# TensorE's program order in the token mix of a two-layer decoder step: where a block's scores stand among the key transposes and the side pieces

## The chip, the cores and the metric

One core of a Trainium2 chip runs the whole step as one program. The metric is the device time of one execution, in microseconds (us), median of several runs.

## What is computed

The reference is a decoder trunk of two layers for a prompt of 256 tokens and for 8 sequences of 8 new tokens each, with 1,024 cached positions per sequence in pages of 128. Each layer is

```
x += 0.5*SwiGLU(RMSNorm(x))
h = RMSNorm(x); project h to queries, keys, values, gates
(A) block-sparse attention, 6 heads: each query keeps the best 3 of the 4 past blocks of 256 keys
(B) forgetting attention, 5 heads: logits get a sum of log forget values
(C) gated linear recurrence, 5 heads
x += concat(A, B, C) @ w_out
x += 0.5*SwiGLU(RMSNorm(x))
```

For the sampled sequences (A) and (B) attend over cached keys and values that are fetched by a page table. The scores of a sequence come in 4 blocks of 256 keys. The softmax of a sequence needs all 4: the sums of the scores pick the block that is left out, and the row maxima give the bias of the exponentials. All of this is in float32.

## The kernel before, in words

The dense products (line 1424) take each weight as a high and a low part. They stand before and after the token mix of each layer, and the change doesn't touch them. The token mix is one unrolled loop over 32 steps, `i` from 0 to 31, on each of TensorE (PE), VectorE (DVE) and ScalarE (ACT). A step is one block of 256 keys: `q, n = divmod(i, 4)`, sequence q, block n of it. Every engine runs its own list of work in exactly the order in which the code gives it, and the lists are tied by semaphores.

TensorE in step i, before the change:

- `turn_keys(i + 1, u)` for u = 0, 1, 2 (line 1588): 12 transposes of cached keys of the next block, 4 in each of three PSUM banks. ACT copies banks 0 and 2 to SBUF (line 688), DVE copies bank 1 (line 1064).
- `block_scores(i)` (lines 1614 and 1618): the scores of this block, into one of four half banks. Blocks 0 and 1 of a sequence write over what the exponentials of the previous sequence read, so block 0 waits until two of its five exponentials are done (line 1614, for line 697).
- n = 1: `turn_weights(q - 1)` (line 1626). n = 2: `values(q - 1)` (line 1643). n = 3: `turn_outputs(q - 1)` (line 1656). These are the previous sequence's softmax weights, its weighted values and its outputs.
- a side piece that belongs to the prompt or to the recurrence. Steps 0 to 13: `prompt_scores(i)` (line 1668), `turn_probs(i - 2)` (line 1680), `prompt_out(i - 3)` (line 1693). Steps 14 to 22: `products(i - 14)` (line 1717). Step 23: `turn_end_keys` (lines 1734 and 1736). Step 24: `rec_own_sums` (line 1748). Steps 25 to 27: state sums, state products and mean squares (line 1795). Steps 28 to 31 have none.

DVE in step i: `block_stats(i - 1)` (lines 1092 and 1093: sum and maximum of the scores), at n = 0 `gates(q - 1)` (lines 1099 to 1105) and `copy_outputs(q - 2)` (line 1143), then `copy_keys(i + 1, 1)` (line 1064), and behind it the work of the side pieces: `prompt_norm(i - 2)`, `prompt_max(i - 1)` (lines 1178 to 1182), `take` and `level_factors` (lines 1223, 1250 and 1251), `level_logs` (line 1244).

ACT in step i: `copy_keys(i + 1, 0)` and `copy_keys(i + 1, 2)` (line 688), then at n = 0 the exponentials `weights(q - 1)` (lines 697 and 699), then `prompt_exp(i - 1)` (line 716), `copy_probs(i - 3)` (line 725), `level_exp` (line 733). ACT's part of the mean squares (lines 760 and 763) stands ahead of its key copies in step 28. In step 23 it copies the cross products (line 748).

So `products(n)` needs DVE's `level_factors(n - 1)` of the same step, `prompt_scores(i)` needs line 1178 of the same step on DVE, and `turn_probs(i - 2)` needs line 725 of the same step on ACT. Each of the three stands behind a key copy of the same step on its engine.

SyncE's queue fetches the key pages (it waits for `keys_turned`), GpSimd's queue the value pages (it waits for `values_used`). The order in which the PSUM banks of the ring are handed out is fixed by `ring_units`, in which block scores don't stand.

Of the kernel before, what the change touches and what calls it, by code (L numbers as in the profile page):

```python
# [239 lines left out]
def trunk(nc, a, outs):  # L240
    ctx = ExitStack()
    with ctx:
# [169 lines left out]
        def settle(eng):  # L412

            eng.sem_inc(waited, 1)
# [998 lines left out]
        def _(te):  # L1413
# [75 lines left out]
            n = DEPTH * 24 + 8  # L1489
# [28 lines left out]
            for L in range(DEPTH):  # L1518
# [38 lines left out]
                def ring(*name):  # L1557

                    if PREVIOUS[name]:
                        te.wait_ge(*was_read(*PREVIOUS[name]))  # L1560
                    settle(te)
                    return ring_bank(*name)
# [16 lines left out]
                def turn_keys(i, u):  # L1579

                    q, n = divmod(i, NBLK)
                    bank = ring(L, "keys", i, u)
                    for j in range(4):
                        a_, pr = divmod(4 * u + j, 6)
                        pg = 2 * n + a_
                        if j == 0 or pr == 0:
                            te.wait_ge(k_in[pg % 4], ((L * DB + q) * 2 + pg // 4) * 32 + 32)
                        last = te.transpose(PS[:, bank, 128 * j:128 * j + 128], key_pages[:, pg % 4, 128 * pr:128 * pr + 128], ident)  # L1588
                    last.then_inc(keys_turned, 1)
# [10 lines left out]
                def block_scores(i):  # L1600

                    q, n = divmod(i, NBLK)
                    Q = L * DB + q
                    for u in range(3):
                        te.wait_ge(*was_read(L, "keys", i, u))
                    if n < 2:
                        if Q:
                            te.wait_ge(weights_ready, 5 * Q - 3 + 2 * n)
                    else:
                        te.wait_ge(block_scores_read, L * BLOCKS + i - 1)  # L1610
                    settle(te)
                    o = [PS[32 * g:32 * g + 32, 3 + n % 2, 256 * (n // 2):256 * (n // 2) + 256] for g in range(3)]
                    for g in (1, 2):
                        te.matmul(o[g], sel[:, q, 32 * g - 32:32 * g], brow[:, 256 * n:256 * n + 256], start=True, stop=False)  # L1614
                    k = keys_t[i % 2][:, :, :].rearrange("p (a j) c -> p j a c", a=2)
                    for m in range(2):
                        for g in range(3):
                            last = te.matmul(o[g], qz[:, q, 2 * g + m, :], k[:, 2 * g + m, :, :], start=g == 0 and m == 0, stop=m == 1)  # L1618
                    last.then_inc(block_scores_done, 1)

                def turn_weights(q):

                    te.wait_ge(weights_ready, (L * DB + q) * 5 + 5)
                    bank = ring(L, "weights", q, 0)
                    for g in range(5):
                        last = te.transpose(PS[:, bank, ROWS * g:ROWS * g + ROWS], weight_rows[:, 128 * g:128 * g + 128], ident[0:ROWS, 0:ROWS])
                    last.then_inc(weights_turned, 1)
                    bank = ring(L, "weights", q, 1)
                    for g in range(3):
                        te.transpose(PS[:, bank, ROWS * g:ROWS * g + ROWS], weight_rows[:, 128 * g + 640:128 * g + 768], ident[0:ROWS, 0:ROWS])  # L1630
                    te.transpose(PS[0:NS, bank, 264:352], new_weights, ident[0:ROWS, 0:ROWS]).then_inc(weights_turned, 1)

                def values(q):

                    Q = L * DB + q
                    for u in range(2):
                        te.wait_ge(*was_read(L, "weights", q, u))
                    bank = ring(L, "values", q)
                    o = [PS[32 * g:32 * g + 32, bank, 0:w] for g, (c, w) in enumerate(GROUPS)]
                    for pg in range(NPG):  # L1640
                        te.wait_ge(v_in[pg], Q * 32 + 32)
                        for g, (c, w) in enumerate(GROUPS):
                            last = te.matmul(o[g], weight_cols[:, pg, 32 * g:32 * g + 32], value_pages[:, pg, c:c + w], start=pg == 0, stop=False, skip_group_check=True)  # L1643
                        last.then_inc(values_used, 1)
                    p, v = [weight_cols[0:NS, NPG, 32 * g:32 * g + 32] for g in range(3)], toks[0:NS, :]
                    te.matmul(o[0], p[0], v[:, 384:640], start=False, stop=True, skip_group_check=True)
                    te.matmul(o[1][:, 0:128], p[1], v[:, 640:768], start=False, stop=True, skip_group_check=True)
                    te.matmul(o[2], p[2], v[:, 3 * 384 + 128:3 * 384 + 320], start=False, stop=True, skip_group_check=True)
                    te.matmul(o[1][:, 128:256], p[1], v[:, 3 * 384:3 * 384 + 128], start=False, stop=True, skip_group_check=True).then_inc(value_sums_ready, 1)

                def turn_outputs(q):

                    te.wait_ge(*was_read(L, "values", q))
                    bank = ring(L, "out", q)
                    for m in range(2):
                        last = te.transpose(PS[:, bank, ROWS * m:ROWS * m + ROWS], out_rows[:, 128 * m:128 * m + 128], ident[0:ROWS, 0:ROWS])
                    last.then_inc(outputs_turned, 1)

                def prompt_scores(h):

                    hf = h % 2
                    r = slice(64 * hf, 64 * hf + 64)
                    qt, kt = pt(T["qa"] + h // 2), pt(T["ka"] + h // 2)
                    if h:
                        te.wait_ge(prompt_scores_read, L * NH + h)
                    for t in range(2):
                        out = PS[:, 5, 128 * t:128 * t + 128 * (t + 1)]
                        last = te.matmul(out, qt[r, 128 * t:128 * t + 128], kt[r, 0:128 * (t + 1)], start=True, stop=h < AH)  # L1668
                        if h >= AH:
                            e = h - AH  # L1670
                            last = te.matmul(out, ident[0:BH, e:e + 1].to_broadcast([BH, 128]), ncn[:, 0:128 * (t + 1)], start=False, stop=True)
                    last.then_inc(prompt_scores_ready, 1)
# [117 lines left out]
                def mean_squares():  # L1790

                    te.wait_ge(rec_squares_ready, L + 1)
                    for j in range(3):
                        bank = ring(L, "squares", j)
                        te.matmul(PS[:, bank, 0:NT], cst("blk"), V_(4, j), start=True, stop=True).then_inc(rec_mean_squares_ready, 1)
# [4 lines left out]
                settle(te)  # L1800
                for i in range(BLOCKS):
                    q, n = divmod(i, NBLK)
                    if i + 1 < BLOCKS:
                        for u in range(3):
                            turn_keys(i + 1, u)
                    block_scores(i)
                    if n == 1 and q >= 1:
                        turn_weights(q - 1)
                    if n == 2 and q >= 1:
                        values(q - 1)  # L1810
                    if n == 3 and q >= 1:
                        turn_outputs(q - 1)
                    if i < NH:
                        prompt_scores(i)
                    if 2 <= i <= NH + 1:
                        turn_probs(i - 2)
                    if 3 <= i <= NH + 2:
                        prompt_out(i - 3)
                    if LEVEL0 <= i <= LEVEL0 + 8:
                        products(i - LEVEL0)  # L1820
                    if i == END0:
                        turn_end_keys()
                    if i == END0 + 1:
                        rec_own_sums()
                    if i == END0 + 2:
                        rec_state_sums()
                        prompt_states()
                    if i == END0 + 3:
                        state_products()
                    if i == END0 + 4:  # L1830
                        mean_squares()
                turn_weights(DB - 1)
                values(DB - 1)
                turn_outputs(DB - 1)
# [57 lines left out]
```

## Time and profile before

| what | value |
|---|---|
| median of 3 runs | 1914.46 us (1908.67 to 1914.79) |
| the profiled execution, device time | 1912.16 us |
| its span, first to last instruction | 1910.5 us |
| TensorE matmul busy | 1755.8 us, 92% |
| VectorE busy | 1100.8 us, 58% |
| ScalarE busy | 638.3 us, 33% |
| mean granted TensorE clock | 0.949 |
| chain that ended last | PE 82%, DVE 10%, ACT 3% |
| lines 1614 and 1618 in that chain | 1% and 2% (block scores) |

A row of the timeline gives the start in us from the span's start, the duration in us, the engine, the line, the operation, what it writes and reads, the shape and the number of instructions merged; in square brackets is the time for which the engine had been idle before it and who ended that. The granted clock is 1.00 at 2.4 GHz and 0.50 at 1.2 GHz.

### The profile page before, as it was taken

To read this page: it belongs to the slowest core of one execution; us is meant where nothing else is said; L and a number is where in the kernel's file an instruction comes from. 1 tells how busy PE (TensorE), PEld (TensorE's weight loads), DVE (VectorE), ACT (ScalarE), POOL (GpSimd) and SP (SyncE) were. 2 spreads that over 40 slices of the span, in tenths; PEclk is the share of its full clock that TensorE was granted. 3 is DMA by queue.
4 is the path that set the end of the run, shared out by engine and by line. 5 is a ranking of instruction groups with operands and counts; after the bars stand their busy time and mean duration, and the time that the engine had idled before them with its cause. 6 is when DMAs were issued, how large, how long until landed. Compare 5 with 4: busy or idle time off the path is not lost.

```text
span 1910.5 us, 33441 instructions
## 1 busy us (share of the span) xinstructions
PE 1755.8 (92%) x12457; PEld 1588.7 (83%) x12457; DVE 1100.8 (58%) x1832; ACT 638.3 (33%) x864; POOL 143.1 (7%) x263
## 2 busy tenths in 40 slices
PE   6999999978998879999999999997889996899997
PEld 5999999955666569999999999996556664899997
DVE  6665564475456456665476655545655544666655
ACT  3333332344323324333343333323432224433332
POOL 0000000011312210000000000001121122000000
PEclk9999999989979889999999999998997788999998
DMA  6444455454635545444544445554554445444443
GB/s 181 152 154 141 151 149 133 129 180 147 197 106 174 164 124 175 145 142 142 162 147 144 152 143 150 148 152 146 151 184 137 130 152 175 147 154 153 145 147 110
DMA packets 284169, 287.31 MB, mean 150 GB/s; under 512 B 26543, under 2 KB 272999, under 8 KB 283943
## 3 DMA queue, kind: packets, MB, share of 16 engines
q1 hardware_dynamic: 268290, 239.53, 41.4%
q0 software_dynamic: 14464, 46.48, 7.8%
q8 instruction: 56, 0.92, 0.2%
q10 hardware_dynamic: 1316, 0.03, 0.1%
q14 instruction: 43, 0.34, 0.1%
HBM read 279.59 MB, written 6.40 MB: 150 GB/s over the span
## 4 chain that ended last, share of the span: by engine, by line
PE 82%; DVE 10%; ACT 3%; issue 2%; DMA 2%; SPq 1%; DVEq 0%; ACTq 0%; POOLq 0%; POOL 0%
PE PS L1424 60%; PE PS L1588 5%; PE PS L1643 3%; PE PS L1717 3%; PE PS L1618 2%; DVE wlo L829 1%; PE PS L1614 1%; DMA raw<-in_ffn_w_gate 1%; ACT weight_rows L697 1%; ACT whi L576 1%; PE PS L1693 1%; PE PS L1721 1%; PE PS L1668 1%; DVE sqsum L844 1%; PE PS L1680 1%
## 5 line engine op out<-in xcount | busy, mean ns | idle before, releaser
L1424 PE MATMUL PS<-xh,whi 128*128 128x320 f32 x1920 | 597.0, 311 | 13.8 <-DMA K<-in_consts 10.2
L1424 PE MATMUL PS<-xl,whi 128*128 128x320 f32 x1920 | 594.4, 310 | 0.0
L1424 PE MATMUL PS<-xh,wlo 128*128 128x320 f32 x1920 | 594.4, 310 | 0.0
L829 DVE TENSOR_TENSOR wlo<-raw,whi 128x2048 fp32r<-128x2048 f32 (+2 forms) x185 | 406.8, 2199 | 263.9 <-ACT whi L576 261.6
L576 ACT ACTIVATE whi<-raw 128x2048 fp32r<-128x2048 f32 (+2 forms) x185 | 340.6, 1841 | 610.5 <-PE PS L1424 603.3
L1424 PEld LDWEIGHTS PS<-xh,whi 128*128 128x128 f32 x1920 | 361.5, 188 | 15.6 <-issue 10.4
L1424 PEld LDWEIGHTS PS<-xh,wlo 128*128 128x128 f32 x1920 | 361.6, 188 | 0.6
L1424 PEld LDWEIGHTS PS<-xl,whi 128*128 128x128 f32 x1920 | 361.4, 188 | 0.0
L1424 PE MATMUL PS<-hh,whi 128*128 128x320 f32 x704 | 217.5, 309 | 0.0
L1424 PE MATMUL PS<-hh,wlo 128*128 128x320 f32 x704 | 217.5, 309 | 0.0
L1424 PE MATMUL PS<-hl,whi 128*128 128x320 f32 x704 | 217.5, 309 | 0.0
L564 POOL DMA_DIRECT2D value_pages<-in_cache_moba_v x128 | 70.2, 548 | 1452.4 <-issue 1068.3
L688 ACT ACTIVATE keys_t<-PS 128x512 f32<-128x512 f32 x128 | 76.3, 597 | 258.2 <-PE PS L1588 258.2
L1424 PEld LDWEIGHTS PS<-hh,whi 128*128 128x128 f32 x704 | 132.1, 188 | 0.0
L1424 PEld LDWEIGHTS PS<-hh,wlo 128*128 128x128 f32 x704 | 132.1, 188 | 0.0
L1424 PEld LDWEIGHTS PS<-hl,whi 128*128 128x128 f32 x704 | 132.1, 188 | 0.0
L1588 PE MATMUL PS<-K,key_pages 128*128 128x128 f32 x768 | 121.4, 317 | 3.8 <-DVE weight_cols L1122 2.2
L1588 PEld LDWEIGHTS PS<-K,key_pages 128*128 128x128 f32 x768 | 103.3, 165 | 18.8 <-issue 13.8
L1064 DVE COPY keys_t<-PS 128x512 f32<-128x512 f32 x64 | 44.2, 691 | 114.7 <-PE PS L1588 114.6
L1618 PE MATMUL PS<-keys_t,qz 128*32 128x256 f32 x768 | 105.4, 413 | 0.0
L866 DVE TENSOR_TENSOR tmp<-PS,rstd 128x320 f32<-128x320 f32 x88 | 42.6, 488 | 89.1 <-PE PS L1424 88.9
L594 ACT ACTIVATE tmp<-tmp 128x320 f32<-128x320 f32 x88 | 40.3, 463 | 115.0 <-DVE tmp L866 115.0
(252 smaller groups left out, 1852.2 us busy)
## 6 DMA issues: line engine op xcount, KB each, us to landing
raw<-in_ffn_w_gate SPq DMA_DIRECT2D x45, 1024.0 KB
raw<-in_ffn_w_up SPq DMA_DIRECT2D x45, 1024.0 KB
raw<-in_ffn_w_down SPq DMA_DIRECT2D x32, 1024.0 KB
raw<-in_w_in SPq DMA_DIRECT2D x64, 512.0 KB
key_pages<-in_cache_moba_k SPq DMA_DIRECT2D x128, 192.0 KB, 2.5
value_pages<-in_cache_moba_v POOLq DMA_DIRECT2D x128, 192.0 KB, 2.9
key_pages<-in_cache_fox_k SPq DMA_DIRECT2D x128, 160.0 KB, 2.6
value_pages<-in_cache_fox_v POOLq DMA_DIRECT2D x128, 160.0 KB, 3.2
```

Source lines behind the costliest of these rows:

```text
L564: pool.dma_start(value_pages[:, pg, 0:AW], vmv[:, ds(page + L * NPOOL, 1), :].rearrange("p a c -> p (a c)")).then_inc(v_in[pg], 16)
L576: act.activation(whi[s][:, 0:nk, :], raw[s][:, 0:nk, :], ACT.Copy).then_inc(hi_done[s], 1)
L594: act.activation(tmp[j][:, :], tmp[j][:, :], ACT.Silu).then_inc(silu_done, 1)
L688: act.activation(keys_t[i % 2][:, 4 * u:4 * u + 4, :], PS[:, bank, :].rearrange("p (j c) -> p j c", j=4), ACT.Copy).then_inc(read_act[bank ...
L829: dve.tensor_tensor(wlo[s][:, 0:nk, :], raw[s][:, 0:nk, :], whi[s][:, 0:nk, :].bitcast(F32), ALU.subtract).then_inc(split_done[s], 1)
L866: dve.tensor_tensor(tmp[j][:, :], PS[:, j, 0:NT], rstd[:, :], ALU.mult).then_inc(gate_scaled, 1)
L1064: dve.tensor_copy(keys_t[i % 2][:, 4 * u:4 * u + 4, :], PS[:, bank, :].rearrange("p (j c) -> p j c", j=4)).then_inc(read_dve[bank], 1)
L1424: last = te.matmul(out, w[wslot][r, kt, cols], x[r, at, :], start=start and n == 0 and m == 0, stop=stop and n == len(ktiles) - 1 and m == 2)
L1588: last = te.transpose(PS[:, bank, 128 * j:128 * j + 128], key_pages[:, pg % 4, 128 * pr:128 * pr + 128], ident)
L1618: last = te.matmul(o[g], qz[:, q, 2 * g + m, :], k[:, 2 * g + m, :, :], start=g == 0 and m == 0, stop=m == 1)
L1643: last = te.matmul(o[g], weight_cols[:, pg, 32 * g:32 * g + 32], value_pages[:, pg, c:c + w], start=pg == 0, stop=False, skip_group_check= ...
L1717: last = te.matmul(PS[:, 5 + at // 2, c:c + 128], kk[r, 128 * t:128 * t + 128], qq[r, 128 * t:128 * t + 128], start=True, stop=True)
```

## The change

Only TensorE's list changes. The scores of a sequence's fourth block (n = 3) go ahead of the transposes of the next block's keys. The scores of a sequence's first block (n = 0, all sequences but the first) go behind the side piece of their step. Blocks 1 and 2, and step 0, stay as they were. Nothing is added or removed, and the lists of the other engines and queues are the same.

```diff
                 for i in range(BLOCKS):
                     q, n = divmod(i, NBLK)
+                    if n == 3:
+                        block_scores(i)
                     if i + 1 < BLOCKS:
                         for u in range(3):
                             turn_keys(i + 1, u)
-                    block_scores(i)
+                    if n in (1, 2) or i == 0:
+                        block_scores(i)
                     if n == 1 and q >= 1:
                         turn_weights(q - 1)
                     if n == 2 and q >= 1:
...
                         state_products()
                     if i == END0 + 4:
                         mean_squares()
+                    if n == 0 and q >= 1:
+                        block_scores(i)
                 turn_weights(DB - 1)
```

## Rows read from the trace of the kernel before

**Rows 1.** Windows, the token mix of either layer: us, busy of each engine, granted clock.
```profile
410.00:690.00 280.00, 234.47 (x1958) 161.25 (x1957) 149.96 (x394) 94.17 (x238) 61.38 (x112) 0.88 0.51 157
1338.00:1620.00 282.00, 240.14 (x1958) 164.93 (x1956) 147.43 (x391) 93.37 (x237) 61.41 (x112) 0.86 0.51 156
```
**Rows 2.** Waits of PE, whole span: us in total, times, longest us.
```profile
PE PS L1614 <- ACT weight_rows L697: 29.0, 14, 3.8
...
PE PS L1668 <- DVE idle L1178: 9.5, 8, 1.7
...
PE PS L1680 <- ACT idle L725: 7.0, 8, 1.6
...
PE PS L1717 <- DVEq L824: 5.9, 4, 1.5
...
PE PS L1736 <- DVE P L1143: 4.4, 2, 2.2
...
PE PS L1717 <- issue: 3.2, 4, 1.2
```
**Rows 3.** Timeline of PE, steps 19 and 20 of the first layer.
```profile
569.61 0.41 PE L1614 MATMUL PS<-brow,sel 80*32 80x256 f32 x2
...
572.88 2.75 PE L1717 MATMUL PS<-b 64*128 64x128 f32 x20 [1.48 <-DVEq L824]
575.57 2.51 PE L1588 MATMUL PS<-K,key_pages 128*128 128x128 f32 x12
579.87 0.41 PE L1614 MATMUL PS<-brow,sel 80*32 80x256 f32 x2 [1.79 <-ACT weight_rows L697]
...
581.29 2.16 PE L1717 MATMUL PS<-b 64*128 64x128 f32 x20
583.37 1.53 PE L1588 MATMUL PS<-K,key_pages 128*128 128x128 f32 x12
```
**Rows 4.** Timeline of DVE: steps 19 and 20, then step 16, then steps 27 and 28.
```profile
569.28 0.69 DVE L1064 COPY keys_t<-PS 128x512 f32<-128x512 f32 x1 [2.59 <-PE PS L1588]
...
572.18 0.55 DVE L1251 TENSOR_TENSOR b<-b,P 128x384 f32<-128x384 f32 x1
...
580.45 0.55 DVE L1251 TENSOR_TENSOR b<-b,P 128x384 f32<-128x384 f32 x1
...
537.64 0.65 DVE L1251 TENSOR_TENSOR b<-b,P 128x480 f32<-128x480 f32 x1
...
641.45 0.69 DVE L1064 COPY keys_t<-PS 128x512 f32<-128x512 f32 x1 [0.33 <-PE PS L1588]
643.36 0.42 DVE L1092 TENSOR_REDUCE gate_sums<-PS 48x1 f32<-48x256 f32 x1 [1.22 <-PE PS L1618]
```
**Rows 5.** Timeline of ACT: step 20, then steps 8 and 12, then step 23.
```profile
578.11 0.60 ACT L688 ACTIVATE keys_t<-PS 128x512 f32<-128x512 f32 x1 [0.80 <-PE PS L1588]
...
579.05 0.47 ACT L697 ACTIVATE weight_rows<-PS,exp_bias 88x256 f32<-88x256 f32 x1
...
469.50 0.49 ACT L725 ACTIVATE idle<-PS 128x384 f32<-128x384 f32 x1
...
501.64 0.49 ACT L725 ACTIVATE idle<-PS 128x384 f32<-128x384 f32 x1
...
600.78 0.50 ACT L748 ACTIVATE idle<-PS 128x384 f32<-128x384 f32 x1
```
**Rows 6.** Timeline of PE: side pieces of steps 4, 8, 12, then step 16.
```profile
435.73 0.52 PE L1680 MATMUL PS<-K,idle 128*128 128x128 f32 x3 [0.15 <-ACT idle L725]
...
471.25 0.55 PE L1680 MATMUL PS<-K,idle 128*128 128x128 f32 x3
...
502.27 0.52 PE L1680 MATMUL PS<-K,idle 128*128 128x128 f32 x3
...
537.03 0.64 PE L1614 MATMUL PS<-brow,sel 80*32 80x256 f32 x2 [1.79 <-ACT weight_rows L697]
...
539.74 0.86 PE L1717 MATMUL PS<-b 64*128 64x128 f32 x4
```

## The prediction

> **What bounds the kernel now.** I read the windows first. The token mix of a layer is about 280 us of a span of 1910.5, and in it PE is busy for 234 of 280 and 240 of 282 us at a granted clock of 0.88 and 0.86 [rows 1]. So TensorE sets the pace, with gaps. Next I read PE's waits, for what fills the gaps [rows 2]. The largest is the one that the change aims at: line 1614, the first block's scores, waits 14 times for ACT's exponentials, 29.0 us. Two of these (step 28 in each layer) are the longest, 3.8 each; the other twelve are 1.79 each, as (29.0 - 7.5) / 12 gives. Then come waits of the side pieces: for DVE's line 1178, for ACT's line 725, for DVE's level factors (put down to "DVEq" and "issue", 5.9 and 3.2 us) and for line 1143. Last I read the timelines of PE, DVE and ACT beside each other, for what each of these waits hangs on, since that is what a reordering moves.
>
> Two links decide. The wait of 1.79 hangs on ACT's order: the last key copy of the step starts at 578.11, as the transposes end, two exponentials follow it, the second from 579.05 on, and PE starts at 579.87 [rows 3, 5]. The waits of the side pieces hang on a key copy too: in step 19 DVE copies keys at 569.28, and behind that copy it takes the level products and makes the factors, to 572.18 + 0.55 = 572.73, and PE's products start 0.15 later, at 572.88, after 1.48 us of idling [rows 3, 4]. That copy can start only once PE has turned the keys. So in steps with such a wait the path is: PE turns keys, DVE (or ACT) copies, DVE works, PE's side piece. The scores, which take 581.29 - 579.87 = 1.42 us [rows 3], run beside DVE's part of that path now and cost nothing.
>
> **Part 1: the fourth block's scores ahead of the key transposes (steps 3, 7, 11, 15, 19, 23, 27).** The transposes, and with them the copy and all that hangs on it, start one scores' length later; what remains between transposes and side piece is nothing or the small line 1656. So the wait grows by what the scores no longer cover. Step 19: the scores from 569.61 on stood inside the 3.6 us between copy and products; now they stand ahead, the products start 1.42 later and the wait goes from 1.48 to 2.9. Steps 3 and 7 have the same through line 1178, step 11 through line 725 (which waits for DVE's maxima behind its copy), step 15 through the factors, step 23 through line 1143, which DVE reaches behind its copy and the end keys [rows 2]. That is +1.42 for five of them. Step 15 runs at the lower clock, where scores take up to 539.74 - 537.03 = 2.71 [rows 6]; between 1.42 and 2.71 I take 1.9, since its clock changes inside the step. The early scores bring nothing in return: DVE does their statistics only behind its copy and the work of the step, and has no wait there to lose; the exponentials start behind ACT's last copy, not at the gates. Step 27 is the exception. There the copy (641.45) is done before the scores, DVE idles 1.22 us for them until 643.36 [rows 4], and from these statistics on the path goes through the mean squares and ACT to the wait of 3.8 in step 28. With the order turned, the copy is at 641.45 + 1.42 = 642.87, ends at 643.56, and the statistics start about 0.1 to 0.2 later than now. So steps 27 and 28 together cost 0.1. Part 1 is 5 x 1.42 + 1.9 + 0.1 = 9.1 us in a layer. Its price is not below 0.1 in any step, and with all six at the higher price it would be 6 x 2.71 = 16.3.
>
> **Part 2: the first block's scores behind the side piece (steps 4, 8, ..., 28).** If the piece could start when the transposes end, it would fill the wait of 1.79. It mostly cannot, since it hangs on the same copies. For each step: the piece ends earlier than now by how long it is ready before its present start, and the scores then add their length on PE's path; the difference is 1.42 less that lead.
> - Step 4: line 1680 starts at 435.73 after idling 0.15 for ACT [rows 6], behind all the exponentials in ACT's list. Lead 0, cost +1.4.
> - Step 8: ACT's line 725 ends at 469.99, PE starts at 471.25 [rows 5, 6]. Lead 1.1 (with 0.15 for the signal), cost +0.3.
> - Step 12: line 725 ends at 502.13, PE starts at 502.27. Lead 0, cost +1.4.
> - Step 16: factors end at 538.29, PE starts at 539.74 [rows 4, 6]. Lead 1.3, but scores of up to 2.71 at the lower clock; between +0.1 and +1.4, and I take +1.3, since the rows of this step are at the lower clock.
> - Step 20: factors end at 581.00, PE starts at 581.29 [rows 3, 4]. Lead 0.1, cost +1.3. PE would idle from 578.1 to 581.15, 3 us at one piece.
> - Step 24: the cross products were copied by 601.28 [rows 5], in the step before. Here the piece, line 1748, is ready and long enough, and the wait of 1.79 goes: -1.8.
> - Step 28: no piece. 0.
>
> Sum 3.9 in a layer. What else hangs on it: scores of block 0 now stand right ahead of the next transposes, and DVE's statistics (0.8 us) are done before the second third of the keys is turned; cost nothing, and 0.1 a step if not. The waits of blocks 0 and 1 for the exponentials get cover, as said. DMAs: the fetches of key pages on SyncE's queue follow the transposes and those of value pages on GpSimd's follow the values, both in the same order and in steps that get longer, so that each has more time than now; cost nothing, and that cover grows with every wait.
>
> **Clock.** The new waits are longer. After the 1.48 us wait of step 19 the next transposes took 2.51 us, those after the 1.79 us wait 1.53 [rows 3]: so some waits bring a stretch at 1.2 GHz and some don't. One such stretch costs up to 2.71 - 1.42 = 1.3 us of PE's path. Some ten waits in a layer get longer. From both sides: no more stretches than now, 0; one behind each, 13 us in a layer. I take 1.5 more in a layer, 2 us, nearer to the low end, because the rows show a like wait with none, and because several of the new waits stand where the clock is already low. The Trainium skill ("TensorE: Matmul & The Clock Gate", Part 1) has it that half speed is the default state and that only activity releases the throttle. By that rule the high end would come; the rows here bear it out in part (a fall behind one wait, none behind the longer one).
>
> **Sum.** 9.1 + 3.9 + 2 = 15 us in a layer, 30 in both, as the second layer runs the same list in a stretch as long [rows 1] and the counts of these waits are even [rows 2]. Against the profiled execution: 1912.2 + 30 = 1942, or 1.6% more. That execution is 2.3 us under the median of the runs shown (1914.46), so on the median's scale it is 1944.5; I forecast 1943.
>
> **Rivals.**
> - *The clock takes the high end:* the same sum with 13 in place of 2: 2 x (13.0 + 13) = 52, so 1964; anything from 1955 to there I count to it. For it: ten waits of up to 3 us. Against: the row above. This is where the rule of the Trainium skill's page would lead. 0.10.
> - *The early scores are free:* if the pieces of steps 3 to 23 were held by something earlier than the copy, part 1 is 0 and 2 x (3.9 + 2) = 12 remain, 1924. Against: DVE's row 569.28 is itself ended by PE's transposes. 0.05.
> - *The piece does fill the wait, part 1 stands:* part 2 is then -1.8 in six steps, -10.7, with part 1 at 9.1: 2 x -1.6 = -3, so 1909, within 0.3%. It needs the factors and line 725 to come without the key copy ahead of them; the rows 580.45 and 501.64 speak against it. 0.03.
> - *Faster, as such an order would be meant:* TensorE's wait of 1.79 is filled in six steps of each layer and the early scores cost nothing: 12 x -1.79 = -21.5, so 1891. Its place is the start of the side piece at n = 0, its price the 1.79, and a step gains once its piece is ready less than 1.79 us after the last transpose. By the rows that is so in step 24 alone. 0.03.
>
> That the order is not taken as written I leave out: the rows of PE follow the code's order.
>
> **How the numbers follow.** The forecast has 0.79, and its own range is 1932 to 1954: down by 10 for no clock loss, 4 us, and 0.2 to 0.3 of slack in each of 24 dearer steps, up by 11 for scores at the lower clock and two more stretches a layer. The whole range, 1930 to 1957, leaves out the last three rivals and most of the first. About 0.3% (5.7 us) is what a measurement of this kernel can tell from no change. Faster by more: 0.03. Within: 0.04, the third rival and a hundredth of the second's low end. Slower by more: 0.93.
>
> **What would show it.** In the changed kernel's profile: (1) the wait of line 1614 for line 697 falls from 14 times to about 2, those of step 28; (2) PE's waits for line 1178, line 725 and the factors grow from 9.5 + 7.0 + 5.9 + 3.2 = 25.6 us [rows 2] to some 65, with single ones of 2.5 to 3.3; (3) in step 19 the products start 3.6 us after DVE's key copy, as before, and the copy itself 1.4 later than the scores' start plus a transpose; (4) step 24 has no wait ahead of scores or own sums; (5) the stretch from 410 on ends some 15 us later; (6) the granted clock of the token mix is 0.02 or so lower. It is wrong if the products of steps 19 and 20 start without a wait, or if PE's total idle time in the mix does not grow.

## The result, and the profile after

The changed kernel takes 1978.35 us (median of 4 runs, 1978.01 to 1979.74) where the kernel before takes 1914.62 in the same comparison: 3.35% slower, ratio 1.0335 with a 95% interval of 1.0303 to 1.0366. The direction was forecast, the size was not: 1943 with a range up to 1957. The profiled execution has a span of 1978.0 us and a mean granted clock of 0.925 (before: 1910.5 and 0.949).

First the windows of the token mix of both layers, from the first transpose of the new scores (line 1597) to the last output transpose (line 1656). The columns are the window, its length, busy time of PE, of PE's weight loads, of DVE, ACT and POOL (with counts), then the granted clock, the DMA share and GB/s. Before:

```profile
408.26:685.44 277.18, 235.26 (x1972) 162.07 (x1971) 147.49 (x388) 93.87 (x237) 61.38 (x112) 0.89 0.52 159
1336.58:1618.54 281.96, 241.32 (x1972) 166.21 (x1971) 147.57 (x388) 93.86 (x237) 61.41 (x112) 0.86 0.51 156
```

After:

```profile
410.98:722.67 311.69, 254.25 (x1971) 173.18 (x1971) 147.45 (x388) 93.80 (x237) 61.43 (x112) 0.82 0.46 141
1373.62:1685.18 311.56, 257.20 (x1972) 175.56 (x1971) 147.31 (x388) 93.78 (x237) 61.51 (x112) 0.81 0.46 141
```

The mix grew by 34.5 and 29.6 us, 64.1 together, so nearly the whole loss of 67.5 us in span is there. It splits in two. TensorE's time without work, length less busy, went from 82.6 to 111.8 us, +29.2. Its busy time went from 476.6 to 511.5, +34.9, for the same matmuls: they ran slower. The granted clock fell from 0.89 to 0.82 and from 0.86 to 0.81. DVE and ACT did the same work in the same time. PE's waits for pages from memory didn't grow (key pages 1.6 to 1.1 us, value pages 1.2 to 1.4 in all), so the loss isn't one of the DMAs.

The waits of PE in the changed kernel, as in [rows 2] (us in total, times, longest):

```profile
PE PS L1717 <- DVEq L824: 32.5, 12, 3.6
PE PS L1668 <- DVE idle L1178: 22.3, 12, 3.2
PE PS L1680 <- ACT idle L725: 18.6, 11, 3.3
...
PE PS L1614 <- ACT weight_rows L697: 7.5, 2, 3.8
...
PE PS L1734 <- DVEq L824: 3.5, 2, 1.7
```

The wait that the change aims at is gone but for step 28: 14 times became 2, 29.0 us became 7.5. In its place the waits of the side pieces for line 1178, line 725 and the factors went from 25.6 to 73.4 us, and step 23 has a wait at line 1734 that was 0.5 us before.

Steps 19 and 20 of the first layer, PE and then DVE, to be laid beside [rows 3, 4]:

```profile
597.26 1.24 PE L1618 MATMUL PS<-keys_t,qz 128*32 128x256 f32 x11
598.43 1.53 PE L1588 MATMUL PS<-K,key_pages 128*128 128x128 f32 x12
...
603.15 2.79 PE L1717 MATMUL PS<-b 64*128 64x128 f32 x20 [2.98 <-DVEq L824]
605.87 2.82 PE L1588 MATMUL PS<-K,key_pages 128*128 128x128 f32 x12
...
611.47 3.92 PE L1717 MATMUL PS<-b 64*128 64x128 f32 x20 [2.77 <-DVEq L824]
615.33 0.63 PE L1618 MATMUL PS<-keys_t,qz 128*32 128x256 f32 x1
...
618.02 1.53 PE L1588 MATMUL PS<-K,key_pages 128*128 128x128 f32 x12
```

```profile
599.56 0.69 DVE L1064 COPY keys_t<-PS 128x512 f32<-128x512 f32 x1 [4.01 <-PE PS L1588]
...
602.43 0.55 DVE L1251 TENSOR_TENSOR b<-b,P 128x384 f32<-128x384 f32 x1
...
607.88 0.69 DVE L1064 COPY keys_t<-PS 128x512 f32<-128x512 f32 x1 [0.83 <-PE PS L1588]
...
610.76 0.55 DVE L1251 TENSOR_TENSOR b<-b,P 128x384 f32<-128x384 f32 x1
```

In step 19 the products start 603.15 - 599.56 = 3.59 us after DVE's key copy, the same as before (3.60), and PE's wait is 2.98 instead of 1.48: the scores left the place where they covered it. Step 20, from transposes to transposes, takes 618.02 - 605.87 = 12.15 us where it took 583.37 - 575.57 = 7.80. Of these 4.35 us the order accounts for 1.3, as worked out in the prediction. The rest is rate, that is, the same matmuls take longer: the products take 3.86 us to the scores' start instead of 2.08, the scores 2.69 instead of 1.42.

What PE did before the clock fell is seen in pairs of neighbouring windows of the changed kernel, same columns:

```profile
430.40:433.80 3.40, 1.75 (x9) 1.13 (x10) 3.12 (x13) 1.36 (x5) 0.00 (x0) 0.99 0.63 200
433.80:437.20 3.40, 3.40 (x16) 2.71 (x14) 0.71 (x2) 0.60 (x1) 0.00 (x0) 0.51 0.00 0
512.30:515.70 3.40, 1.05 (x7) 0.76 (x7) 3.13 (x13) 1.36 (x5) 2.14 (x5) 1.00 0.90 292
515.70:519.10 3.40, 3.16 (x15) 2.44 (x13) 1.86 (x9) 0.80 (x2) 0.73 (x2) 0.50 0.76 268
601.00:604.40 3.40, 1.25 (x14) 1.28 (x15) 3.09 (x7) 0.27 (x1) 2.10 (x5) 1.00 0.95 268
604.40:618.00 13.60, 10.83 (x56) 8.27 (x55) 6.54 (x20) 4.94 (x16) 1.27 (x3) 0.50 0.43 145
```

Each first row holds one of the new waits and is granted 2.4 GHz (1.00, once 0.99); each second row is work behind it at 1.2 GHz (0.50, once 0.51). The first rows hold the waits of steps 3, 11 and 19, or their ends.

### The profile page after: what moved, and what is told of

Same layout as the page of the kernel before. It is cut to its first block and busy times, and to the rows that moved or that the text cites. A ratio compares the mean times of both kernels' runs of the same rounds, so it can differ in the third digit from the quotient of the medians.

```text
span 1978.0 us, 33441 instructions
## 1 busy us (share of the span) xinstructions
PE 1793.0 (91%) x12457; PEld 1611.4 (81%) x12457; DVE 1100.7 (56%) x1832; ACT 638.5 (32%) x864; POOL 143.3 (7%) x263
## 5 line engine op out<-in xcount | busy, mean ns | idle before, releaser
L1588 PEld LDWEIGHTS PS<-K,key_pages 128*128 128x128 f32 x768 | 109.4, 173 | 29.2 <-issue 26.0
L1588 PE MATMUL PS<-K,key_pages 128*128 128x128 f32 x768 | 128.1, 330 | 3.5 <-DVE weight_cols L1122 2.4
L1618 PE MATMUL PS<-keys_t,qz 128*32 128x256 f32 x768 | 112.2, 435 | 0.0
L1717 PE MATMUL PS<-b 64*128 64x128 f32 x280 | 56.4, 377 | 32.5 <-DVEq L824 32.5
```

The lines of the kernel that those rows point to most:

```text
L1717: last = te.matmul(PS[:, 5 + at // 2, c:c + 128], kk[r, 128 * t:128 * t + 128], qq[r, 128 * t:128 * t + 128], start=True, stop=True)
```

## The experiments

All times are medians, set against runs of the kernel before on the same chip (medians of 1911 to 1915 us). The ratio is taken from all runs and not from the two medians, and differs from theirs by up to 0.2%. Kernels whose times are set against each other below may have run on different chips, so that a difference of 3 us between them says nothing. A theory stood against rivals at first. Theory **A**: the side pieces hang on the key copies, so the new order makes the waits longer, and the longer waits bring the lower clock. **The rivals**: the loss sits in one half of the change, or the slow rate comes of the order or of the small matmuls themselves and not of the waits.

| kernel | us | ratio to before, 95% interval |
|---|---|---|
| fourth block's scores early, alone | 1944.5 | 1.017, 1.0126 to 1.0213 |
| first block's scores late, alone | 1948.0 | 1.019, 1.0145 to 1.0236 |
| the change, waits filled | 1933.0 | 1.0119, 1.0063 to 1.0175 |
| before, waits filled | 1898.4 | 0.9939, 0.9912 to 0.9967 |
| the change, DVE's key copy late | 1934.8 | 1.013, 1.0078 to 1.0182 |
| before, DVE's key copy late | 1890.4 | 0.9897, 0.9853 to 0.9941 |
| before, all key copies late | 1865.7 | 0.9768, 0.9731 to 0.9805 |
| the same, fourth block's scores early | 1871.6 | 0.9795, 0.9753 to 0.9837 |
| the same, first block's scores late | 1913.9 | 1.002, 1.0001 to 1.004 |
| the change, all key copies late | 1918.9 | 1.0044, 1.0017 to 1.007 |
| step 24's scores late, alone | 1911.0 | 0.9996, 0.9974 to 1.0017 |
| all key copies late, and step 24's scores late | 1867.9 | 0.9765, 0.9736 to 0.9794 |

**One half at a time.** The first edit keeps the early scores and puts block 0's back:

```diff
                     if n == 3:
                         block_scores(i)
...
-                    if n in (1, 2) or i == 0:
+                    if n != 3:
                         block_scores(i)
...
-                    if n == 0 and q >= 1:
-                        block_scores(i)
```

> Only the first half of the change: the fourth block's scores ahead of the key transposes. Theory A (the side pieces hang on key copies; the longer waits then bring the lower clock, at a little over one us of slower work for each us of added wait): added idle time 9 us in a layer, and with the clock about 35 to 45 us in all, so 1950 to 1960. Rival B (most of the loss comes of the first block's scores standing last in their step): under 1930.

The second keeps block 0's late scores and puts the fourth block's back:

```diff
-                    if n == 3:
-                        block_scores(i)
...
-                    if n in (1, 2) or i == 0:
+                    if n != 0 or i == 0:
                         block_scores(i)
```

> Only the second half: the first block's scores behind the side piece. Theory A: added idle 4 us in a layer and with the clock 15 to 25 us in all, so 1930 to 1940, and the waits of line 1614 for line 697 gone but for those of step 28. Rival B: 1950 or more.

Measured: 1944.5 and 1948.0, so +30.5 and +34.0 over the 1914.0 of their comparison. They add up to the whole (64.5 against 64). Neither guess of the split was right: the first is under its 1950 to 1960, the second above its 1930 to 1940. Rival B, most of the loss in the late scores, doesn't hold either: both halves cost about the same. The windows show how each loss is made up, first the early scores alone, then the late scores alone:

```profile
408.88:703.00 294.12, 241.37 (x1971) 165.84 (x1971) 147.56 (x388) 93.58 (x237) 61.23 (x112) 0.86 0.49 150
1354.41:1648.83 294.42, 243.39 (x1972) 166.44 (x1971) 147.41 (x388) 93.57 (x237) 61.32 (x112) 0.86 0.49 149
```

```profile
411.77:706.50 294.73, 248.96 (x1971) 169.08 (x1971) 147.48 (x388) 93.77 (x237) 61.20 (x112) 0.84 0.49 149
1357.35:1651.53 294.18, 248.90 (x1971) 169.21 (x1971) 147.57 (x388) 93.78 (x237) 61.24 (x112) 0.84 0.49 150
```

Against before, the early scores add 21.2 us of idling and 8.2 of busy time; the late scores add 8.5 of idling and 21.3 of busy time. The idle parts are close to what the prediction gave its two parts (18.2 and 7.8 for both layers). The rate is a cost of its own and isn't in proportion to the added idling. Longer single waits don't explain that. The lines of the factors' wait, early scores and then late scores:

```profile
PE PS L1717 <- DVEq L824: 19.5, 8, 3.6
```

```profile
PE PS L1717 <- DVEq L824: 22.1, 10, 3.4
```

The longest waits for line 1178 and line 725 are 3.2 and 3.1 us with the early scores, 2.5 and 3.3 with the late ones, so that the kernel with the smaller loss of rate has waits as long. Why the late scores cost so much more rate stays open.

**Is it the waits that bring the lower clock?** Useless matmuls fill them. They write into the PSUM bank that is handed out next, once its last reader is done; `FILL` gives their number by step:

```diff
+FILL = {3: 10, 4: 8, 7: 11, 8: 4, 11: 11, 12: 11, 15: 11, 16: 11, 17: 7, 19: 11, 20: 10, 21: 5, 23: 6}
...
+                def fill_wait(i):
+                    if i in FILL:
+                        te.wait_ge(*was_read(L, "keys", i + 1, 0))
+                        settle(te)
+                        bank = ring_bank(L, "keys", i + 1, 0)
+                        for _ in range(FILL[i]):
+                            te.matmul(PS[:, bank, 0:128], ident, cst("perm"), start=True, stop=True)
...
                     if n in (1, 2) or i == 0:
                         block_scores(i)
+                    fill_wait(i)
```

> The changed kernel with idle waits filled: in 13 steps of each layer 4 to 11 more float32 matmuls of 128 rows and 128 columns stand right behind the key transposes, written into the ring bank that is next free and overwritten later; they take less than the wait in which they stand. Theory A (the lower clock is the waits' doing): granted clock of the token mix back to 0.90 or more, time down by 15 to 35 us, so 1943 to 1963, although TensorE does more. Rival C (the slower work comes of the new order or of the side pieces' small matmuls, not of the waits): clock as in the changed kernel, 0.80 to 0.82, and time the same or above, 1978 to 1985.

Measured: 1933.0. The change with 116 useless matmuls more in each layer is 45 us faster than without them, more than theory A's range of 15 to 35. Windows:

```profile
408.12:695.07 286.95, 256.56 (x2203) 184.76 (x2203) 147.53 (x388) 93.61 (x237) 61.25 (x112) 0.92 0.50 154
1346.70:1632.49 285.79, 257.44 (x2204) 185.73 (x2203) 147.50 (x388) 93.61 (x237) 61.22 (x112) 0.91 0.50 154
```

The clock is at 0.92 and 0.91, above that of the kernel before. Order, side pieces and links are those of the changed kernel; only what PE does in the waits differs. So the slow rate is the waits' doing, and rival C falls. That the gain went past the range is probably because the fills also stand in for waits that the kernel before had already; no run separates the two. The same on the kernel before shows what its own waits cost:

```diff
+FILL = {2: 4, 3: 4, 4: 7, 7: 6, 8: 7, 11: 6, 12: 7, 15: 4, 16: 7, 19: 6, 20: 7, 21: 6, 24: 7}
```

> The kernel before with its own waits filled in the same way: 4 to 7 matmuls of 128 rows and columns in 12 steps of each layer, in waits of 1.2 to 1.8 us. Theory A (waits bring the lower clock, also before the change): granted clock above 0.949, about 0.965, and 5 to 20 us faster than before, 1895 to 1910. Rival C (only the long waits of the changed kernel do): clock as before and time the same or up to 5 us more for the matmuls that stick out.

Measured: 1898.4, by the medians 16 us faster than before, by the ratio's interval 6 to 17. The fills are 78 matmuls in each layer; they stand in 13 steps (not 12, as expected), ahead of the scores at n = 0 and behind them elsewhere. Windows:

```profile
409.06:682.85 273.79, 248.66 (x2128) 176.22 (x2127) 147.30 (x388) 93.77 (x237) 61.20 (x112) 0.91 0.52 161
1334.32:1602.76 268.44, 243.76 (x2128) 173.28 (x2127) 147.54 (x388) 93.78 (x237) 61.23 (x112) 0.93 0.54 164
```

The clock of the two filled kernels is nearly the same, and with both filled the change costs 1933.0 - 1898.4 = 34.6 us instead of 64. That is near the 29.2 us that its idling alone had grown by. So of the 64 us some 30 are the clock's share; this is an estimate, since the two kernels hold different numbers of fills.

**Do the waits hang on the key copies?** The copy on DVE goes behind the side pieces' work, TensorE's list stays:

```diff
-                    if i + 1 < BLOCKS:
-                        copy_keys(i + 1, 1)
...
                     if LEVEL0 <= i <= LEVEL0 + LEVELS:
                         level_logs(i - LEVEL0)
+                    if i + 1 < BLOCKS:
+                        copy_keys(i + 1, 1)
```

> The changed kernel with one more reordering, on VectorE alone: its key copy of a step stands behind prompt norm, prompt maxima, level products and level factors instead of ahead of them; TensorE's list is the changed one. Theory A (the new waits hang on that copy): the waits of line 1668 for line 1178 and of line 1717 for the factors nearly vanish, and the time falls by 50 us or more, to 1905 to 1925. Rival D (they hang on the length of VectorE's work or on signals, not on the copy's place): within 10 us of the changed kernel, 1968 or more.

Measured: 1934.8, 44 us less, so the link is real and rival D falls, but it is short of the 50 us or more and above the range. PE's waits:

```profile
PE PS L1680 <- ACT idle L725: 23.2, 10, 3.3
PE PS L1630 <- DVE keys_t L1064: 13.9, 7, 2.9
...
PE PS L1717 <- DVEq L824: 7.7, 4, 2.5
```

Those for line 1178 are no longer among the large ones and those for the factors fell from 32.5 to 7.7 us. Two things take their place. ACT's own copy still stands ahead of line 725; and the second half of the transposes of the softmax weights (line 1630) needs the PSUM bank that the late copy frees. The same edit on the kernel before:

> The kernel before with VectorE's key copy of a step behind the work of the side pieces, TensorE's list as before. Theory A: the waits for line 1178 and for the factors go (18.6 us in both layers), new ones may come where the second half of the weights' transposes (line 1630) needs the bank that the copy frees; 10 to 25 us faster, 1890 to 1905. Rival D: the same within 5 us.

Measured: 1890.4, 24 us faster, at the low end of the range. Next, ACT's copies go behind the exponentials and line 725 as well:

```diff
-                    if i + 1 < BLOCKS:
-                        copy_keys(i + 1, 0)
-                        copy_keys(i + 1, 2)
...
                     if 3 <= i <= NH + 2:
                         copy_probs(i - 3)
+                    if i + 1 < BLOCKS:
+                        copy_keys(i + 1, 0)
+                        copy_keys(i + 1, 2)
```

> As before_dve_late, and ScalarE's two key copies of a step behind the exponentials and line 725 too. Theory A: the waits of line 1614 for line 697 and of line 1680 for line 725 go as well; 20 to 45 us faster than before, 1870 to 1895. Rival: the waits only move to the copies that now come late (lines 1626, 1630 and the next block's scores), within 10 us of before_dve_late.

Measured: 1865.7, 2.3% faster than the kernel before and just past the range. This kernel beats both. The wait of line 1614, for which the change was made, goes here from the side of its releaser: 29.0 us became 5.6, and line 1630's new wait is 6.7.

```profile
PE PS L1630 <- DVE keys_t L1064: 6.7, 4, 2.6
...
PE PS L1614 <- ACT weight_rows L697: 5.6, 2, 2.8
```

**With the link cut, is the new order free?** The whole change and then its halves on top of the late copies:

> The changed kernel with the key copies late on both VectorE and ScalarE, so it differs from before_both_late (1865.7) only in TensorE's order, by the very change of this study. Theory A (the fourth block's early scores cost because the pieces hang on copies of keys turned later; with the copies late that link is gone, but the first block's scores then lose their cover where turned weights or a side piece wait for the late copies): slower than before_both_late by 10 to 40 us, 1875 to 1905, and faster than before. Rival E (once no piece hangs on a key copy the new order is free or better): 1860 to 1868.

Measured: 1918.9, 53 us above the 1865.7 and even above the kernel before. The order costs nearly as much as ever, which the range (up to 1905) did not have, and rival E (the order free or better) is as far off. So the link over the copy cannot be the cause of all of it. Which half it is:

> before_both_late (1865.7) with the first half of the change alone: the fourth block's scores ahead of the key transposes. Theory A (that half costs through the link from the key transposes over the copy to the side piece; the link is gone here): within 8 us of before_both_late, 1862 to 1874, where the same edit cost 30 us with the copies early. Rival F (it costs for another reason): 15 us or more above it, 1881 or more.

> before_both_late with the second half alone: the first block's scores behind the side piece. Theory A: the exponentials are done before the piece is ready, since VectorE's statistics and gates stand ahead of the piece's work in every first block's step, so the scores leave a wait unfilled that they filled before: most of the 53 us, 1900 to 1915. Rival F: 15 us or less above before_both_late, under 1881.

Measured: 1871.6 and 1913.9, both inside theory A's ranges. With the copies late, the early scores cost 6 us where they cost 30, and the intervals of the two ratios (0.9731 to 0.9805 and 0.9753 to 0.9837) overlap, so that these 6 us may be none; that half does act through key transposes, copy and piece. The late scores cost 48: in the mixes of both layers 21.1 us of idling and 20.9 of busy time. One reason shows in step 20 of the change with late copies, PE, then DVE, then ACT:

```profile
582.09 3.92 PE L1717 MATMUL PS<-b 64*128 64x128 f32 x20 [2.50 <-DVEq L824]
585.95 0.63 PE L1618 MATMUL PS<-keys_t,qz 128*32 128x256 f32 x1
```

```profile
578.03 0.79 DVE L1143 COPY P<-PS 64x24 f32<-64x24 f32 x4
579.10 1.65 DVE L1223 COPY_PREDICATED idle<-K,PS 128x512 f32<-128x512 int32 x3 [0.28 <-DVE P L1143]
...
581.38 0.55 DVE L1251 TENSOR_TENSOR b<-b,P 128x384 f32<-128x384 f32 x1
```

```profile
578.61 0.46 ACT L697 ACTIVATE weight_rows<-PS,exp_bias 88x256 f32<-88x256 f32 x1
```

The second exponential ends at about 579.1, so the scores could start while PE idles 2.50 us up to 582.09. They stand in PE's list behind the products, and these wait for DVE, which in a first block's step does the statistics, the gates and the output copies before it comes to the products' work. In this step the scores are the early work and the side piece is the late one, with the key copy ahead or behind. The change put them the wrong way round.

A second reason lies one step later, where the late scores hold up the engines that read them. Step 5 with late copies and late scores alone, DVE, ACT, PE:

```profile
436.85 0.42 DVE L1092 TENSOR_REDUCE gate_sums<-PS 48x1 f32<-48x256 f32 x1 [4.98 <-PE PS L1618]
```

```profile
441.73 1.06 ACT L688 ACTIVATE keys_t<-PS 128x512 f32<-128x512 f32 x2
```

```profile
442.41 0.57 PE L1626 MATMUL PS<-K,weight_rows 88*128 88x88 f32 x5 [2.73 <-issue]
```

DVE begins a step with the statistics of the last scores, and here it idles until they are there. Its maxima for the prompt follow them, then ACT's exponentials, line 725 and the key copies, and line 1626 writes into the bank that the first of these copies reads. So the key copies start 441.73 - 436.73 = 5.00 us after the step's first transpose, where they start 432.31 - 429.37 = 2.94 us after it with the late copies and the scores in their old place, and PE's wait at line 1626 is 2.73 us instead of 0.66. In both layers the waits of line 1626 for which the profile names no releaser rose from 1.3 to 8.9 us by the late scores, those of line 1717 from 5.1 to 13.1.

**The one step in which the order is right.** Only step 24's scores go behind the own sums:

```diff
-                    block_scores(i)
+                    if i != END0 + 1:
+                        block_scores(i)
...
+                    if i == END0 + 1:
+                        block_scores(i)
```

> The kernel before with one move alone: in step 24 the scores stand behind the own sums, the one step in which the side piece is ready when the transposes end. Theory A: 1.8 us less idling a layer, so 1 to 6 us faster with the clock, 1909 to 1913. Rival (the move costs there too): 3 us or more slower.

Measured: 1911.0 against 1914.2, but the ratio's interval (0.9974 to 1.0017) includes no change, so no gain is shown. The wait itself went as expected:

```profile
PE PS L1614 <- ACT weight_rows L697: 25.4, 12, 3.8
```

12 instead of 14 times and 3.6 us less, two waits of 1.8. On top of the late copies it was to bring nothing:

> before_both_late with step 24's scores behind the own sums. With the exponentials ahead of ScalarE's copies there is no wait left in step 24 for the piece to fill. Theory A: the same as before_both_late within 3 us. Rival: 2 to 6 us faster.

Measured: 1867.9 against 1865.7, the same.

## Why the prediction was wrong, point by point

*Direction and mechanism: right.* It named the two links (exponentials behind ACT's last key copy; side pieces behind a key copy) and said that the scores lose their place beside DVE's path. Step 19's wait was to be 2.9 us and is 2.98, step 20's was to be 3 and is 2.77; the distance from DVE's copy to the products stayed at 3.6; line 1614 waits twice, as said. Part 1 and part 2 gave 26 us of added idling in both layers, and it was 29.2. The waits of the side pieces were to total 65 us and total 73.4. In step 23 the path was named wrong though its size was right: the wait for line 1143 stayed at 2.2 us, and line 1734 waits 1.7 us instead.

*The step that failed is the clock.* It took "1.5 more in a layer, 2 us", 4 us in all, between bounds of 0 and 13 a layer. PE's busy time grew by 34.9 us in the two mixes. Even the high bound was too low (26 in all), for two reasons that the rows show. A stretch at 1.2 GHz behind a wait was priced at one unit's loss, 1.3 us, but the one behind step 19's wait lasts at least 13.6 us, through the transposes, the next wait, the products and the scores. The trace of the kernel before has a stretch as long, behind a wait of 1.20 us in step 15, PE and then the window:

```profile
525.44 0.68 PE L1717 MATMUL PS<-b 64*128 64x128 f32 x4 [1.20 <-issue]
```

```profile
526.40:540.00 13.60, 11.81 (x53) 8.41 (x54) 7.90 (x24) 4.87 (x15) 0.00 (x0) 0.50 0.31 102
```

It holds most of step 15's products, the transposes, the 1.79 us wait of step 16 and its scores, which the prediction read for their price alone [rows 6]. And the choice within the bounds was made from one pair of rows, of waits of 1.48 and 1.79 us, for waits that were to be 2.5 to 3.3 us, outside what these rows cover. The rule of the Trainium skill ("TensorE: Matmul & The Clock Gate", Part 1), that half speed is the default and activity releases it, pointed at the high end and was nearer than my choice: with the waits filled the clock of the mix rose from 0.82 and 0.81 to 0.92 and 0.91. The forecast that the clock would be 0.02 lower failed with it; it fell by 0.07 and 0.05. So did the 15 us by which the first layer's mix was to grow; it grew by 34.5.

*The rivals.* The first, the clock at its high end, was the right one in kind, at 0.10, and 1964 was still too low. None of the others came true; the faster one fails where the prediction said, at pieces that aren't ready.

*Step 27 and 28, step 24.* Step 28's wait is 3.75 as before, so that its 0.1 us stood. Step 24 lost its wait.

*What the prediction missed about part 2.* It put the late start of the side piece down to the key copies alone. With the copies late on both engines the late scores still cost 48 us: in step 20 the statistics, gates and output copies also stand ahead of the piece's work on DVE. That DVE's statistics come later was put at nothing. With the key copies early the profile shows no wait at line 1626 behind it; with the copies late it cost a part of the 7.6 us of new waits there.

## What to carry to other kernels

In this kernel work that covered a wait cost nothing where it stood. Before such work is moved, ask what it covers and who waits to read it, and of two pieces that both wait, put first the one whose input comes first. The key copies were the links, and moving them on the engines that release TensorE took 2.3% off, where moving TensorE's own work added 3.4%. Price a new wait of TensorE twice, once for its length and once for the work behind it at the lower clock; in this kernel the second was the larger, 34.9 against 29.2 us, and a fill of useless matmuls gave 45 us back.

## What was not expected of the hardware

Adding work to a wait made the program faster: 78 useless matmuls in 13 steps of each layer took 16 us off the kernel before (ratio 0.9939, interval 0.9912 to 0.9967), and 116 took 45 off the changed one. And the cost in rate was not in proportion to the idling: the early scores added 21.2 us of idling and 8.2 of slower work, the late scores 8.5 and 21.3. Why the second kind does so much more harm for each us is open: its longest waits are about as long as those of the first (3.4 and 3.6 us), and no run varies where in the step they stand.
